# The low part of the w_gate chunks moved two tiles further on in GpSimd's program

## What is computed

```python
mix = neighborhood_attention(x, na_w_qkv, na_rpb, na_w_o)      # ends with  out @ w_o
x   = layer_norm(DN_ALPHA * x + mix, ln1_g, ln1_b)
hid = jnp.square(jax.nn.relu(x @ w_ff1))
ple = jax.nn.sigmoid(x @ w_ple_gate) * (p @ w_ple_proj)
x   = layer_norm(DN_ALPHA * x + hid @ w_ff2 + ple, ln2_g, ln2_b)
```

## Time and profile before

| | |
|---|---|
| median of 3 runs | 1280.46 us (1279.86 to 1280.94) |
| the profiled execution | 1279.78 us, of which 1278.0 us from first to last instruction |
| PE busy | 1234.4 us, 97% of the span |
| PEld busy | 1033.3 us, 81% |
| DVE busy | 858.7 us, 67% |
| ACT busy | 578.2 us, 45% |
| POOL busy | 131.9 us, 10% |
| mean granted TensorE clock | 0.987 of full speed |

### The profile page before, as it was taken

The page is one execution under the profiler, slowest core; times in us unless marked ns, Lnnn a source line. Parts: engine busy times, 40 slices in busy tenths (PEclk is TensorE's granted clock), DMA queues, the critical chain, the costliest instruction groups (busy, mean ns, idle before and its releaser), DMA issues.

```text
span 1278.0 us, 17719 instructions
## 1 busy us (share of the span) xinstructions
PE 1234.4 (97%) x5864; PEld 1033.3 (81%) x5864; DVE 858.7 (67%) x1702; ACT 578.2 (45%) x1107; POOL 131.9 (10%) x82
## 2 busy tenths in 40 slices
PE   7999999999999895899999999999999999999997
PEld 6888888888888784678888888888888888888886
DVE  4477677777777645556777676676655575588786
ACT  4355655555657722112335444444445433333671
POOL 0211211211223423220000000000000000000000
PEclk9999999999999997889999999999999999999999
DMA  8323223223225671516544444344459678668543
GB/s 194 93 60 82 56 70 85 54 71 86 53 84 160 214 194 57 148 64 225 175 136 152 148 165 148 141 164 156 135 199 350 253 277 300 226 228 302 204 119 99
DMA packets 139342, 195.75 MB, mean 153 GB/s; under 512 B 10496, under 2 KB 72832, under 8 KB 139264
## 3 DMA queue, kind: packets, MB, share of 16 engines
q1 hardware_dynamic: 139264, 194.80, 47.1%
HBM read 136.04 MB, written 50.52 MB: 146 GB/s over the span
## 4 chain that ended last, share of the span: by engine, by line
PE 91%; ACT 2%; DVE 2%; issue 1%; POOL 1%; DMA 1%; SPq 0%; DVEq 0%; ACTq 0%
PE bank L2436 24%; PE bank L2404 23%; PE bank L1101 18%; PE bank L1231 7%; PE bank L2360 6%; PE bank L1185 3%; PE bank L1164 3%; PE bank L1147 3%; PE bank L1123 3%; DMA x_tokens<-in_x 1%; POOL attention_tile_lo L717 1%; POOL gate_w_lo L221 1%; PE bank L1139 1%; DMA ple_embedding<-v_T 0%; PE bank L1114 0%
## 5 line engine op out<-in xcount | busy, mean ns | idle before, releaser
L786 ACT ACTIVATE probabilities<-negated_scores,negated_max 128x384 f32<-128x384 f32 (+1 forms) x128 | 75.8, 592 | 141.0 <-DVE negated_max L993 140.6
L1101 PE MATMUL bank<-act_T_hi,w_qkv_hi 128*128 128x512 f32 x336 | 133.6, 398 | 0.0
L1101 PE MATMUL bank<-act_T_lo,w_qkv_hi 128*128 128x512 f32 x336 | 133.5, 397 | 0.0
L1101 PE MATMUL bank<-act_T_hi,w_qkv_lo 128*128 128x512 f32 x336 | 131.9, 392 | 0.0
L974 DVE TENSOR_TENSOR prob_T_lo<-bank,prob_T_hi 128x256 fp32r<-128x256 f32 (+2 forms) x160 | 69.2, 449 | 68.9 <-ACT prob_T_hi L777 67.3
L2404 PE MATMUL bank<-x_combination,weight_parts 128*128 128x512 f32 x480 | 112.8, 389 | 0.1
L2404 PEld LDWEIGHTS bank<-x_combination,weight_parts 128*128 128x128 f32 x480 | 90.0, 188 | 19.1 <-DVE hidden_staging L2143 0.5
L664 POOL TENSOR_TENSOR w_qkv_lo<-weight_raw,w_qkv_hi 128x1024 fp32r<-128x1024 f32 x21 | 50.5, 2402 | 268.3 <-ACT w_qkv_hi L731 268.3
L2436 PE MATMUL bank<-weight_parts,weight_parts_early 128*128 128x512 f32 x312 | 73.0, 389 | 0.0
L2436 PE MATMUL bank<-weight_parts 128*128 128x512 f32 x312 | 73.0, 389 | 0.0
L2436 PE MATMUL bank<-x_combination,weight_parts 128*128 128x512 f32 x312 | 73.0, 389 | 0.0
(11 more groups left out here) (244 smaller groups left out, 2883.8 us busy)
## 6 DMA issues: line engine op xcount, KB each, us to landing
hidden_combinations<-hidden_staging SPq DMA_DIRECT2D x112, 256.0 KB, 2.0
w_ff_in<-in_w_ff SPq DMA_DIRECT2D x27, 1024.0 KB, 7.7
weight_raw<-in_w_ff SPq DMA_DIRECT2D x25, 1024.0 KB, 5.4
weight_raw<-hidden_combinations SPq DMA_DIRECT2D x14, 1024.0 KB, 5.5
hidden_in<-hidden_combinations SPq DMA_DIRECT2D x14, 1024.0 KB, 5.6
weight_raw<-in_na_w_qkv SPq DMA_DIRECT2D x24, 512.0 KB, 4.5
bias_in<-rpb_rows SPq DMA_DIRECT2D x256, 6.0 KB
attention_T<-out_T SPq DMA_DIRECT2D x8, 512.0 KB, 2.9
```

Of the source, the lines that this page charges most:

```text
L786: nc.scalar.activation(prob[:, u % 4, 0:n], score[:, u % 2, 0:n], ACT.Exp, scale=-1.0, bias=nmax[:, u % 4:u % 4 + 1], accum_out=total[:, u ...
L1101: mm = nc.tensor.matmul(proj_ps[gi % 2][:, :], w[wp][:, (par + kind) % 2, k, :], S.act[ap][:, k, t * HALF:(t + 1) * HALF], start=(i == 0), ...
```

## The change

Only POOL's program changes. The low parts of chunks 0, 1 and 2 were behind the low part of attention tiles 2, 3 and 5; they are now behind that of tiles 4, 5 and 7. Chunk 3 stays in tile 7, behind chunk 2. ACT's and SP's programs and all the semaphores' counts stay.

```diff
@@ in tile(t, par, nth) of the program of gpsimd @@
                     nc.gpsimd.tensor_tensor(o_part[1][:, par, :, :], o_raw[:, par, :, :],
                                             o_part[0][:, par, :, :].bitcast(F32), ALU.subtract).then_inc(o_lo, 1)
-                if t in GATE_SPLIT_TILE:
-                    gate_low(nc, pool, nc.gpsimd, S, 0, GATE_SPLIT_TILE.index(t))
+                if t - 2 in GATE_SPLIT_TILE:
+                    gate_low(nc, pool, nc.gpsimd, S, 0, GATE_SPLIT_TILE.index(t - 2))
                 if t == GROUPS - 1:
                     gate_low(nc, pool, nc.gpsimd, S, 0, 3)
```

## The result

The changed kernel takes 1250.05 us (median of 4 runs, 1249.98 to 1251.17), the kernel before 1280.16 us in the same comparison (4 runs, 1278.41 to 1280.94). The ratio is 0.9769, with a 95% interval of 0.9752 to 0.9786: it is faster by 30.1 us. The forecast was 1251.4 us.

A forecast was written before the change was run, and what follows sets the result against it. PE, busy 97% of the span, was taken as the bound, losing time at the output projection. Savings of 9.98 + 9.24 + 9.89 = 29.1 us from 1280.46 gave 1251.4 us, range 1249.4 to 1257.5.

The forecast's parts named there:

- The cause: Output projection: PE waited 21.9 us for attention low parts queued on POOL behind chunks whose high parts came later.
- The sum: Output projection: savings of 9.98, 9.24 and 9.89 us at tiles 3, 4 and 6, together 29.1 us.
- The clock term: Matmuls behind the three waits: about 7.2 us lost to granted clock 0.50, counted as regained.
- The moved POOL instructions at no cost: Three chunk low parts on POOL, 2.35 to 3.10 us each, would move later and cost nothing.
- The SP queue: SP's loads of chunks 2 and 3: their waits for moved low parts are covered by 5 us or more.
- The low part of chunk 3: POOL after tile 7: cover before the gate stage reads chunk 3 at k = 6 stays unchanged, cost nothing.
- The thin cover at tile 2: DVE's layer norm of tile 2 would be ready 2 us before PE wants its rows, the thinnest cover.
- The kinder of the two orders: Layer norm of tiles 3 and 5: rows ready about 9 us behind the tile, against 10 at worst.
- B: Rival: a late layer norm or operand stops PE once or twice, giving back 2 to 6 us: 1253 to 1257; chance 0.13.
- C: Rival: the waits go but the clock does not come back, 21.9 us won: 1258.6 us; chance 0.03.
- D: Rival: something other than the chunks held the attention low parts, no time moves: 1280.5 us; chance 0.03.
- E: Rival: POOL delays DVE's layer norm, each of five turns over 5.8 us late in tiles 3 to 7: above 1280.5; chance 0.01.

The follow-up runs named there:

- Experiments 1 to 3: Kernel before, POOL's order changed so only attention tile 3, 4 or 6 has no chunk ahead of its low part: 1270.2, 1269.74 and 1270.44 us.
- experiment 6: Kernel before, with the low parts of chunks 0, 1 and 2 moved by one tile only, behind tiles 3, 4 and 6: 1250.29 us, ratio 0.9778.
- experiment 4: Kernel before, its waits kept, with PE carrying out 30 idle matmuls in each wait before tiles 3, 4 and 6: 1273.19 us, ratio 0.9948.
- experiment 9: Changed kernel with the low part of attention tile 6 made five times in a row: 1253.58 us, ratio 0.9803.
- experiment 8: Changed kernel with the low part of chunk 0 carried out three times in a row: 1251.55 us, ratio 0.9786.

## Why the prediction was right, point by point

**The cause** (an order, not a lack of POOL time): right. Experiments 1 to 3 show each place by itself, experiment 6 shows that a chunk ahead of an attention tile costs nothing where its high part is not late.

**The sum** of 9.98 + 9.24 + 9.89 us: the stage gave 29.0. The traces of the runs that free one tile gave 9.46, 10.14 and 9.49 us. What differs is the products of the tiles that still stand behind a wait: with A4 freed they took 13.12 and 12.94 us where before it was 13.43 and 13.58, with A3 freed 13.26 and 13.74 for 12.92 and 13.58, with A6 freed 13.67 and 13.05 for 13.43 and 12.92. That the sum meets the stage to 0.1 us is in part luck, since this scatter alone is up to 1 us. The time gained 30.1 us, 1 us more than forecast; 0.8 us of that is the scatter ahead of the stage.

**The clock term** of 7.2 us: right in size, and shown apart from the waits by experiment 4, though not all of it is the clock. With the clock at 1.00 the three tiles took 11.20, 11.19 and 11.19 us in place of 13.43, 12.92 and 13.58, which is 6.35 us. The other 0.8 us, from there to 10.92, goes with the wait itself: in experiment 9 a wait of 2.42 us at full clock left the same 11.18.

**The moved POOL instructions at no cost**: right. The SP queue behaved as reckoned. The loads of chunks 2 and 3 went out at 494.12 and 505.90, right behind the x loads at 493.54 and 505.31, so neither waited for a low part: G0 had ended at 487.46 and G1 at 499.76, over 6 us earlier. The low part of chunk 3 kept its cover as forecast, but that cover is thinner than the one called the thinnest: it ended at 543.52, and PE reached k = 6 of the gate products near 544.7.

**The thin cover at tile 2**: right in kind, about right in size. DVE's timeline after, for tiles 2 and 3, answers to the earlier trace rows:

```profile
485.51 3.03 DVE L287 SCALAR_TENSOR_TENSOR x_tile<-x_tile,ln_mean_var,act_places 128x1024 f32<-128x1024 f32 x1
488.65 1.42 DVE L295 SCALAR_TENSOR_TENSOR x_tile<-x_tile,ln_mean_var,act_places 128x512 f32<-128x512 f32 x2
...
494.59 2.92 DVE L287 SCALAR_TENSOR_TENSOR x_tile<-x_tile,ln_mean_var,act_places 128x1024 f32<-128x1024 f32 x1
497.61 3.36 DVE L295 SCALAR_TENSOR_TENSOR x_tile<-x_tile,ln_mean_var,act_places 128x512 f32<-128x512 f32 x2
```

At tile 2 the rows were ready at 488.65 + 1.42 = 490.1 and PE turned them at 492.6, so 2.5 us were to spare where 2 had been reckoned. For tile 3 they were ready at 501.0, which is 8.2 us behind its products (492.8); 9 to 10 had been reckoned. The kinder of the two orders named there is the one that happens: L287 gets in between the two POOL operations (A5 ends at 496.43, L287 at 497.51), and G1 takes 3.39 us for it. What the forecast had missed about this cover is that PE needs only half of the rows at first, which experiment 8 brought out. The prediction's sentence that the wide steps end when a POOL operation ends is loose: they run their own length behind it. L287 beside G3 ended at 574.43, 1.1 us behind G3 (573.35). Its sums do add that length.

**The rivals.** B, C and D did not come: PE has no wait from 480 to 540, the clock is 1.00, and the time moved. E was far off: three G0 in a row, at the one place with the thin cover, cost 1.2 us of the stage, where E needed 5.8 us at each of five.

## What to carry to other kernels

When an engine with a fixed program order stands idle although its next input but one is ready, look at what it waits for. A step whose input comes later than that of its follower belongs behind the follower, and here one place was enough. Price such a wait from period to period of the bound engine and not by its idle time alone: a quarter of this gain lay in the slower products behind the waits, most of it by the lower clock. Before moving work, find the two or three covers that it thins and write down how many us each has; here they were 2.5 us (layer norm of tile 2), 6 us and more (SP's queue) and 8.5 to 9 us (from the end of A4, A5 or A6 to PE's start on the tile).

## What the runs showed of the hardware

After PE had waited 7.2 to 7.5 us, the granted clock was 0.50 from the first of the products and came back within the tile; the 48 matmuls took 12.9 to 13.7 us. After 3.8 to 4.1 us it was 0.50 from the first product at one tile, and at two it was at first full and then fell to 0.50; they took 12.8 us each time. After 0.98 and 2.42 us, and after the 0.45 to 0.74 us that 30 idle matmuls left, it stayed at 1.00 and they took 10.9 to 11.2 us. So filling half of a wait won nothing that can be measured, and filling nearly all of it won all of the clock.

DVE and POOL took turns in this stage: a DVE step that reads two operands in SBUF waited for the end of the POOL operation under way, then ran ahead of POOL's next one, which was longer by that (3.39 in place of 2.41 us). The two L295 steps took 1.42 us alone, 3.36 us with one such hold and 5.48 us with two. DVE steps that read a bank (L1073 at 0.67 to 0.69 us) kept their time beside POOL.
